# A three-layer network of norms and matmuls: reciprocal root and addend of a layer's output in PSUM, and two shifts in the work of ScalarE at a change of layer

## The reference

```python
def rms_norm(x, gain):
    x32 = x.astype(jnp.float32)
    y = x32 * lax.rsqrt(jnp.mean(x32 * x32, axis=-1, keepdims=True) + RMS_EPS)
    return (y * gain.astype(jnp.float32)).astype(x.dtype)
...
    for layer in range(DEPTH):
        ...
        x = x + rms_norm(y, g[1])
        y = memory_cross_attention(rms_norm(x, g[2]), mem_n, xa_w_q[layer], xa_w_kv[layer], xa_w_o[layer])
        x = x + rms_norm(y, g[3])
        y = swiglu_ffn(rms_norm(x, g[4]), ffn_w_gate_up[layer], ffn_w_down[layer])
        x = x + rms_norm(y, g[5])
```

## Time and profile before

| | us |
|---|---|
| median of 3 runs (lowest to highest) | 2484.34 (2480.78 to 2485.1) |
| profiled execution, its own time | 2486.96 |
| its span, first to last instruction | 2485.6 |
| PE busy | 2391.0 (96%) |
| PE weight loads busy | 2016.2 (81%) |
| DVE busy | 1016.8 (41%) |
| ACT busy | 877.7 (35%) |
| POOL busy | 1072.2 (43%) |
| mean granted clock of PE | 0.982 of full |

### The profile page before, as it was taken

One profiled execution on the slowest core, in us unless ns is written; L12 is line 12 of the kernel. 1 busy time (PEld: TensorE's weight loads), 2 busy tenths in 40 slices (PEclk: granted clock), 3 DMA queues, 4 the chain that ended last, 5 costly groups with the idle time before them and its releaser, 6 DMA issues.

```text
span 2485.6 us, 31067 instructions
## 1 busy us (share of the span) xinstructions
PE 2391.0 (96%) x12860; PEld 2016.2 (81%) x12860; DVE 1016.8 (41%) x1529; ACT 877.7 (35%) x1275; POOL 1072.2 (43%) x811
## 2 busy tenths in 40 slices
PE   7999999999999999999999999998899999999997
PEld 6766877788888887778778888888898998899886
DVE  3236713622210623757236222105574445754403
ACT  4324523422222424755234222224244233322321
POOL 6422743344455442028433444553344443544452
PEclk9999999999999998999999999998899999999999
DMA  4211421223233221014212223332211222322232
GB/s 156 85 59 56 140 93 51 77 95 100 94 102 102 86 93 51 1 60 145 84 52 85 93 93 96 100 101 85 69 35 60 85 94 62 101 95 94 95 107 70
DMA packets 64012, 211.40 MB, mean 85 GB/s; under 512 B 8832, under 2 KB 13056, under 8 KB 63872
## 3 DMA queue, kind: packets, MB, share of 16 engines
q1 hardware_dynamic: 59120, 206.00, 25.4%
q10 hardware_dynamic: 4752, 3.42, 0.5%
HBM read 207.29 MB, written 2.10 MB: 84 GB/s over the span
## 4 chain that ended last, share of the span: by engine, by line
PE 84%; DVE 11%; ACT 3%; issue 2%; DMA 1%; ACTq 0%; POOL 0%; SPq 0%; DVEq 0%
PE ps L406 67%; PE ps L512 5%; DVE u_lo L1492 2%; DVE x L1507 2%; PE ps L734 1%; PE ps L829 1%; PE ps L750 1%; PE ps L755 1%; DVE arena L1505 1%; DMA w_land<-in_units 1%; PE ps L670 1%; PE ps L778 1%; PE ps L863 1%; PE ps L650 1%; DVE acc L1543 1%
## 5 line engine op out<-in xcount | busy, mean ns | idle before, releaser
L2133 POOL TENSOR_TENSOR w_lo<-w_land,w_hi 128x512 fp32r<-128x512 f32 x768 | 1027.2, 1363 | 1321.5 <-ACT w_hi L959 1320.9
L406 PE MATMUL ps<-u_hi,w_hi 128*128 128x512 f32 (+3 forms) x2560 | 826.3, 349 | 40.8 <-DVE u_lo L1492 21.5
L406 PE MATMUL ps<-u_lo,w_hi 128*128 128x512 f32 (+3 forms) x2560 | 819.8, 347 | 0.0
L406 PE MATMUL ps<-u_hi,w_lo 128*128 128x512 f32 (+3 forms) x2560 | 816.5, 345 | 0.0
L406 PEld LDWEIGHTS ps<-u_hi,w_hi 128*128 128x128 f32 x2560 | 460.6, 191 | 116.3 <-DVE u_lo L1492 27.4
L959 ACT ACTIVATE w_hi<-w_land 128x1024 fp32r<-128x1024 f32 x384 | 400.9, 1050 | 337.7 <-DMA w_land<-in_units 330.4
L406 PEld LDWEIGHTS ps<-u_lo,w_hi 128*128 128x128 f32 x2560 | 458.0, 190 | 61.9 <-issue 1.4
L406 PEld LDWEIGHTS ps<-u_hi,w_lo 128*128 128x128 f32 x2560 | 458.8, 191 | 60.3
L406 PE MATMUL ps<-hid_hi,w_hi 128*128 128x512 f32 (+1 forms) x594 | 220.2, 371 | 0.0
L406 PE MATMUL ps<-hid_lo,w_hi 128*128 128x512 f32 (+1 forms) x594 | 219.7, 370 | 0.0
L406 PE MATMUL ps<-hid_hi,w_lo 128*128 128x512 f32 (+1 forms) x594 | 219.4, 369 | 0.0
(11 more groups left out here) (305 smaller groups left out, 2829.0 us busy)
## 6 DMA issues: line engine op xcount, KB each, us to landing
w_land<-in_units SPq DMA_DIRECT2D x384, 512.0 KB, 3.3
x<-in_xT SPq DMA_DIRECT2D x4, 528.0 KB, 7.7
arena<-in_memT ACTq DMA_DIRECT2D x2, 1024.0 KB, 5.5
outT<-x SPq DMA_DIRECT2D x16, 128.0 KB, 1.7
arena<-in_masks ACTq DMA_DIRECT2D x1, 448.0 KB, 3.4
arena<-in_consts ACTq DMA_DIRECT2D x1, 296.0 KB, 3.8
consts<-in_consts SPq DMA_DIRECT2D x1, 256.0 KB, 7.7
arena<-in_consts ACTq DMA_DIRECT2D x1, 256.0 KB
```

The source lines that it names most:

```text
L406: ins = pe.matmul(ps[:, bank, at:at + c1 - c0], w, rhs(k, c0, c1)[which], start=first and h == 0, stop=last and h == 2)
L2133: pool.tensor_tensor(w_lo[:, u % LAND, half], w_land[:, u % LAND, half], w_hi[:, u % RING, half].bitcast(F32), ALU.subtract).then_inc(*uni ...
```

## The change

It touches five changes of layer (p = 1, 2, 4, 5, 6) and no other work:

1. `HALF_BANK`: ACT's Exp writes the 1 / rms of each half into a PSUM bank (4, for p = 6 bank 6) in place of `rstd_y`, and DVE's multiply reads it there. For p = 1, 2, 4, 5 the multiply also writes its product (the addend) into the upper half of bank 4 in place of `y`, and the add reads it there. A multiply then waits for the add before it, since the addend has one buffer.
2. Where `LAST` is 2, ACT makes the fifth unit of the next layer's weights between the first and second square, and no more behind the fifth `u_hi` of the second half.
3. `SQ_SPLIT`: for norms 6 and 7 the squares of tiles 1, 3, 5, 7 go to PSUM, half of the columns in bank 6 and half in bank 7, and the sum reads them there. Those of tiles 2, 4, 6 stay in `sq`.

```diff
@@ -233,7 +233,13 @@
+        HALF_BANK = {1: 4, 2: 4, 4: 4, 5: 4, 6: 6}
+        half_rstd = lambda p, w: ps[:, HALF_BANK[p], 0:w]
+        half_addend = lambda p, w: ps[:, HALF_BANK[p], S // 2:S // 2 + w]
...
+        SQ_SPLIT = (6, 7)
@@ -986,7 +992,10 @@
-                act.activation(s_, x[:, k, a:z], ACT.Square).then_inc(*x_sq.up())
+                v = x[:, k, a:z]
+                if n in SQ_SPLIT and k % 2:
+                    s_, v = ps[:, 6:8, 0:(z - a) // 2], v.rearrange("p (b n) -> p b n", b=2)
+                act.activation(s_, v, ACT.Square).then_inc(*x_sq.up())
@@ -1019,13 +1029,11 @@
-                rsqrt_mean(("y", p, 1), [Y_HALVES[p][1]], D, rstd_y, rstd_y_at)
+                rsqrt_mean(("y", p, 1), [Y_HALVES[p][1]], D, rstd_y, rstd_y_at, half_rstd(p, width(1)))
                 for k in range(DT):
                     upper_step(n, k, 1)
                     if steps and k == 0:
                         steps()
-                    if k == 4 and LAST[p] == 2:
-                        hi_to(UNIT[following] + 5)
                 for k in range(DT):
                     if k in (1, 3):
                         hi_to(UNIT[following] + 5 + k // 2)
@@ -1499,9 +1507,15 @@
-                addend, r = (y_, rstd_y[:, c0:c1]) if p in Y_HALVES else (ps[:, AT_ADDEND, 0:S], ps[:, AT_RSTD, 0:S])
+                if p not in Y_HALVES:
+                    addend, r = ps[:, AT_ADDEND, 0:S], ps[:, AT_RSTD, 0:S]
+                else:
+                    addend = half_addend(p, c1 - c0) if HALF_BANK.get(p) == 4 else y_
+                    r = half_rstd(p, c1 - c0) if p in HALF_BANK else rstd_y[:, c0:c1]
                 if k and p not in Y_HALVES:
                     dve.wait_ge(*x_new.at(added(p, k - 1)))
+                elif (k or h) and HALF_BANK.get(p) == 4:
+                    dve.wait_ge(*x_new.now())
@@ -1540,7 +1554,10 @@
-                        dve.tensor_tensor(acc[:, c0:c1], acc[:, c0:c1], s_, ALU.add).then_inc(*x_sum.up())
+                        sum_ = acc[:, c0:c1]
+                        if n in SQ_SPLIT and k % 2:
+                            s_, sum_ = ps[:, 6:8, 0:(c1 - c0) // 2], sum_.rearrange("p (b n) -> p b n", b=2)
+                        dve.tensor_tensor(sum_, sum_, s_, ALU.add).then_inc(*x_sum.up())
```

More of the change, by code:

```diff
@@ L1009, in out_and_norm @@
                     copy(o, 0)
-                rsqrt_mean(("y", p, 0), [Y_HALVES[p][0]], D, rstd_y, rstd_y_at)
+                width = lambda h: Y_HALVES[p][h][1] - Y_HALVES[p][h][0]
+                rsqrt_mean(("y", p, 0), [Y_HALVES[p][0]], D, rstd_y, rstd_y_at, half_rstd(p, width(0)) if p in HALF_BANK else None)
                 if not following:
```

## The result

| | before | after |
|---|---|---|
| median (lowest to highest), us | 2484.72 (2480.78 to 2487.03), 4 runs | 2466.26 (2464.64 to 2469.24), 4 runs |
| profiled execution, its span | 2486.96, 2485.6 | 2464.64, 2463.3 |
| mean granted clock of PE | 0.982 | 0.989 |

The ratio is 0.9926, 95% interval 0.9903 to 0.9948: 13 to 24 us less. The forecast was 2470, the range 2464 to 2479. The same kernel was timed again with the experiments: 2468.65 (6 runs, 2464.68 to 2474.5) beside 2482.36 for before (23 runs, 2476.18 to 2491.8), ratio 0.9949 (0.9932 to 0.9965). Both intervals hold 12.9 to 16.9 us, and so the 14.2 that was forecast; the first pair of medians alone would say 18.5.

The account below looks back on a forecast made before the run. PE's chain (84%) bounds the kernel, waiting for DVE at changes of layer. 3.4 + 3.4 + 0.85 + 3.4 + 1.1 + 2.0 = 14.2 us off 2486.96 gives 2472.8; the median lies 2.6 lower: 2470 us, range 2464 to 2479.

Parts of the forecast that it names:

- What bounds: At the changes of layer PE waits for DVE's `u_lo` (21.5 us in 22 waits); POOL delays DVE instructions with two SBUF inputs.
- Operands at zero cost: Multiplies and adds using bank 4 (p = 1, 2, 4, 5) keep their times without POOL, 479 and 425 ns.
- the surcharge: Rival, chance 0.06: each PSUM operand holds DVE longer, 7.4 us on 128 instructions; gain 6.8 us, 2477.5.
- the same bank: Rival, chance 0.07: multiplies reading and writing bank 4 take 262 ns more, 64 times; 7.7 us slower, 2492.
- The unit of weights, 1.9 + 1.9 + 2.0: Moving the unit at p = 1, 4, 6 removes DVE's 2.04 us of stretching and PE's waits: 1.9, 1.9, 2.0 us.
- T2, 0.85: Change of layer p = 2: the add no longer meets POOL, the `u_lo` behind still does; 0.85 us gained.
- T5, 3.4 to the mean: Change of layer p = 5: operands give 0.85 us, squares in PSUM shorten the sums by 2.6; 3.4 us by the mean.
- T1 and T4, 3.4: Changes of layer p = 1 and 4: 3.4 us gained each, full clock included, the sums then being last at the mean.
- T6, 2.0: Change of layer p = 6: the gain is PE's 2.0 us of waiting in the second half.
- Taken as even: At p = 6 the unit among the squares costs 1 us, sums reading PSUM give up to 0.9 us back.
- The clock: Half rate behind waits goes: 1.7 us each at p = 1 and 4, 1.1 us more behind p = 5's mean.
- The wait for the add, 0.12 us where no `u_lo` stands between: In a half's first two tiles the multiply starts some 0.12 us later; 0.7 us in all.

Follow-up runs that it names:

- r2: Changed kernel with the unit of weights back behind the fifth upper part of the second half at p = 1, 4, 6; 2472.81 us.
- r3: Changed kernel with 1 / rms and addend of the halves back in SBUF, without the multiply's wait for the add; 2470.90 us.
- r5: Kernel before, with each of POOL's two subtractions of a unit cut in two (256 columns in place of 512); 2479.30 us, ratio 0.9978.
- r4: Changed kernel with all squares of norms 6 and 7 back in the SBUF buffers; 2474.46 us.
- r9: Kernel before, unedited, run once more for a second profile; one run, 2477.93 us.
- r1: Changed kernel, unedited, timed again with a second profile; 2468.65 us.
- r10: Changed kernel, unedited, run once more for a third profile; one run, 2469.82 us.

## Why the prediction was right, point by point

*What bounds.* That PE waits for DVE at the changes of layer, and that the SBUF operands beside POOL make DVE late, held. "The instructions that take one tensor from PSUM don't show it" held: none of the 128 moved to bank 4 took over 0.50 us. But with the unit moved only 8 of them, at T2 and T5, have POOL beside them; that those at T1 and T4 are shielded too is shown by r2, where 8 there have POOL beside them too (and one multiply of T6). After the change, groups of instructions by form (busy us, mean ns of one, idle before):

```profile
L1521 DVE TENSOR_TENSOR x<-x,ps 128x256 f32<-128x256 f32 x64 | 26.9, 420 | 2.2
L1519 DVE SCALAR_TENSOR_TENSOR ps<-arena,vecs,ps 128x256 f32<-128x256 f32 x32 | 15.5, 484 | 4.4 <-ACT ps L975 4.2
L1519 DVE SCALAR_TENSOR_TENSOR ps<-y_ffn,vecs,ps 128x256 f32<-128x256 f32 x32 | 15.4, 482 | 4.6 <-ACT ps L975 4.4
...
L1519 DVE SCALAR_TENSOR_TENSOR arena<-arena,vecs,ps 128x256 f32<-128x256 f32 x8 | 3.8, 474 | 0.3 <-ACT ps L975 0.3
```

*Operands at zero cost.* Right: 482 to 484 and 420 ns against 479 and 425. It fells two rivals, the surcharge (as an estimate from the Trainium skill, VectorE: DVE Perf Modes, the section on the TRN2 errata, 65 ns each: not seen) and the same bank, whose ends were 0 and 262 ns: reading and writing bank 4 in one instruction costs at most some 10 ns (482 and 484 ns, beside 474 at T6, where the product goes to SBUF).

*The unit of weights, 1.9 + 1.9 + 2.0.* The sum was right, its owner wrong at T1 and T4. The step said that DVE's 2.04 us go with the unit's move. r2 shows that without the move the PSUM operands keep 2.90 and 3.05 of 3.3 and 3.5 us, r3 that the move without PSUM operands keeps all. The two parts do the same work twice, and the move's own share is 0.4 and 0.5 us there, 1.0 at T6. The signs named for it came: after the change PE has no wait over 0.5 us in the second halves of T1, T4 and T6 and none for the lower part of the weights there, and the clock is full.

*T2, 0.85.* Too small by 0.55 us, the term of the sum that was mis-sized most; 1.40 was measured. The step took the `u_lo` behind the add at 1.3 us. It took 0.78, and the next 0.66 (DVE and POOL, after):

```profile
818.25 2.71 POOL L2150 TENSOR_TENSOR w_lo<-w_land,w_hi 128x512 fp32r<-128x512 f32 x2 [10.59 <-ACT w_hi L965]
...
819.05 0.78 DVE L1500 SCALAR_TENSOR_TENSOR u_lo<-x,vecs,u_hi 128x256 fp32r<-128x256 f32 x1
...
820.60 0.66 DVE L1500 SCALAR_TENSOR_TENSOR u_lo<-x,vecs,u_hi 128x256 fp32r<-128x256 f32 x1
```

An instruction beside POOL isn't slowed by a factor; it starts about 1.10 us from the start of POOL's piece (which the profile gives 1.28 us): 458.71 + 1.09 at T1 before, 818.25 + 1.10 here (819.05 + 0.30). What it pays is the rest of the piece, and only if it comes second: at T2 before, a multiply began 0.07 us ahead of POOL's piece and was not held, and the add behind it was (1.38 us):

```profile
821.57 0.48 DVE L1505 SCALAR_TENSOR_TENSOR y_ffn<-y_ffn,vecs,rstd_y 128x256 f32<-128x256 f32 x1
821.64 2.96 POOL L2133 TENSOR_TENSOR w_lo<-w_land,w_hi 128x512 fp32r<-128x512 f32 x2 [10.59 <-ACT w_hi L959]
```

The first two instructions of the tile no longer wait, so the third comes late in the piece. The Trainium skill has this rule (SBUF — State Buffer, the section on its two separate sides): a VectorE instruction with two SBUF inputs and a GpSimd instruction that reads SBUF exclude each other for a whole instruction. The trace agrees, with these numbers and those of r5.

*T5, 3.4 to the mean.* 3.41 to 3.49. Its two parts, one too small and one too large: operands 1.40 (r4; 0.85 was taken), squares 1.95 (r3; 2.6 was taken, since 9.0 us, not 8.5, lie from the first square at 1690.67 to the last sum's end at 1699.70). Errors of opposite sign, so that 3.4 came out is luck. PE's wait for the sums is 0.77 us where under 0.6 was named. Of the three sums from `sq` one took 1.86 us and two 0.80, where two long ones were expected:

```profile
1690.67 0.63 ACT L998 ACTIVATE acc<-x 128x528 f32<-128x528 f32 x1
...
1693.59 1.86 DVE L1560 TENSOR_TENSOR acc<-acc,sq 128x528 f32<-128x528 f32 x1
...
1699.00 0.70 DVE L1560 TENSOR_TENSOR acc<-acc,ps 128x528 f32<-128x528 f32 x1
```

*T1 and T4, 3.4, "the sums take over as the last one there".* The number was right (3.29 and 3.51), this step was not:

```profile
465.39 3.86 DVE L1560 TENSOR_TENSOR acc<-acc,ps 128x512 f32<-128x512 f32 x5 [0.52 <-ACT ps L998]
```

T1's sums end at 469.25, and PE comes to the mean 0.58 us later, at 469.83, without a wait; at T4 it is 0.20 us. PE itself came 3.3 us earlier at T1 and 3.5 at T4, not the 3.6 taken for it. One reason is on record: the half-rate stretch was worth 1.5 us (r9), not 1.7.

*T6, 2.0.* 1.77 measured. "Taken as even" hid two terms, the unit among the squares and the squares in PSUM, that cancel: without the split T6 is at −0.20.

*The clock.* Behind T5 1.1 us was taken. Half rate there fell from 6.8 us to 3.4, its loss from 3.4 to 1.7 us, in all three profiles of after, and was 6.8 us long in r3, r4 and r9. Not all of that loss was time: from T5's mean to PE's first matmul of the next stage (L850, now L856) before took 1780.04 − 1716.82 = 63.2 us, after 1761.82 − 1699.76 = 62.1 (63.1 in r9, 61.9 and 62.1 in r1 and r10). That is 1.1 us, as taken. With it the marks give 14.5 us against the first profile of before.

```profile
1780.04 0.30 PE L850 MATMUL ps<-consts,arena 128*16 128x2 f32 x6 [4.47 <-DVE arena L1932]
```
```profile
1761.82 0.29 PE L856 MATMUL ps<-consts,arena 128*16 128x2 f32 x6 [4.09 <-DVE arena L1949]
```

At T1 and T4 the stretches came off the first profile, but r9 shows that T4's isn't there in every execution: against the second profile of before the same edits gave 11.9 us by the marks of the five changes. So the mechanism of this term (no wait, no half rate) held, and that both stretches were there to be gained was luck. So was the closeness of the total: T2 was 0.55 us too small, T1 and T6 together 0.3 too large.

*The wait for the add, 0.12 us where no `u_lo` stands between*: 0.46 us from the add's start to the multiply's at T5's second half (1681.32 to 1681.78), 0.34 before. Right, and worth 0.05 us at T1 and T4 (r3).

## To carry to other kernels

Where DVE leads and POOL works beside it, count only the instructions with two SBUF inputs that come while POOL's is under way, and price each by what is left of it. One operand in PSUM took that price away here (0.42 and 0.48 us); POOL instructions half as long halved it for each but not in all (1.88 us beside 2.04). Two remedies for one stall don't add up: undo each alone before it is given credit. And compare stages between marks of an unchanged engine: here one profile against another could be off by 5 us in a part that nobody touched.

## What the hardware showed that was not expected

That a multiply may read and write one PSUM bank for at most 10 ns more. That half rate behind a wait of 1.96 to 1.99 us is neither certain nor rare (3 of 4 at T1 and T4, 0 of 2 at T6; behind the waits of 1.72 to 1.75 us in the first halves of T1, T4 and T6 it came 14 times of 27), and never began in the second halves of T1 and T4 without the wait (0 of 20). One such stretch in a first half cost nothing up to the last mark: T1 of before took 36.46 us with it and 36.47 without. And that a stage with the same instructions (marks 847.86 to 1129.33) took between 276.15 and 284.78 us in the thirteen profiles; in the five of before and after the granted clock from 969 to 1000 us lay anywhere between 0.61 and 0.92.
